# A hybrid attention and convolution layer: the last nine taps of one channel tile move from VectorE to ScalarE products with adding DMAs

## What is computed

```
h    = modulate(rms_norm(x)),  proj = h @ w_in
q, k, v -> 8 heads of windowed attention with 2 key groups, 256 context keys, a sink
u    = ga * sigmoid(gb)                       # 512 channels
u    = silu(layer_norm(depthwise_conv(u)))    # 31 taps, centred, over positions
x    = x + g1 * (concat(attn, u) @ w_out)
x    = x + g2 * ((silu(gate) * val) @ w_down) # gate, val: w_up with 3 taps
shift, scale, gate of both halves: silu(c) @ w_mod + b_mod   (w_mod 1024 x 6144)
```

## Time and profile before

| | |
|---|---|
| median of 3 runs | 1235.33 us |
| the profiled execution | 1237.15 us, its span 1235.3 us |
| mean granted PE clock | 0.964 |
| PE busy | 1159.9 us (94%) |
| DVE busy | 948.4 us (77%) |
| ACT busy | 580.2 us (47%) |
| POOL busy | 315.4 us (26%) |
| head groups 0 to 15 | 243.9 to some 463 us |

### The profile page before, as it was taken

One profiled execution on the slowest core, in us unless ns is written; L12 is line 12 of the kernel. 1 busy time (PEld: TensorE's weight loads), 2 busy tenths in 40 slices (PEclk: granted clock), 3 DMA queues, 4 the chain that ended last, 5 costly groups with the idle time before them and its releaser, 6 DMA issues.

```text
span 1235.3 us, 16863 instructions
## 1 busy us (share of the span) xinstructions
PE 1159.9 (94%) x5837; PEld 962.4 (78%) x5837; DVE 948.4 (77%) x1403; ACT 580.2 (47%) x993; POOL 315.4 (26%) x335
## 2 busy tenths in 40 slices
PE   5799999889999999998799999999999998999997
PEld 1378888788888987786588888788788876888885
DVE  0479988679984454458999999999999967788687
ACT  4452356765545563545443444434444434444441
POOL 2100011134563000000544453635520000002256
PEclk9899999989899879999899999999999998999998
DMA  9322555519999013222445445355342285335352
GB/s 376 109 73 71 130 103 114 143 33 258 266 261 273 2 53 110 105 76 69 154 130 176 152 136 170 120 169 158 131 153 78 76 320 200 103 104 159 102 162 85
DMA packets 102833, 174.90 MB, mean 142 GB/s; under 512 B 9322, under 2 KB 62690, under 8 KB 101748
## 3 DMA queue, kind: packets, MB, share of 16 engines
q1 hardware_dynamic: 84692, 112.04, 27.1%
q0 software_dynamic: 16928, 57.88, 18.9%
q10 hardware_dynamic: 1152, 4.19, 0.9%
HBM read 116.41 MB, written 30.41 MB: 119 GB/s over the span
## 4 chain that ended last, share of the span: by engine, by line
PE 36%; DVE 12%; issue 5%; ACT 4%; DMA 3%; POOL 1%; DVEq 0%; ACTq 0%; SPq 0%; POOLq 0%
PE ps L1527 16%; PE ps L1492 5%; PE ps L1577 5%; PE ps L1578 5%; PE ps L1579 5%; DVE y L1931 2%; DVE w_op L1830 2%; DMA hid<-hid_scratch 2%; DVE w_raw L1848 1%; DVE y L1927 1%; ACT y L1722 1%; ACT w_op L1642 1%; POOL p_all L2099 1%; DVE u L1920 1%; DVE s_sum L1848 1%
## 5 line engine op out<-in xcount | busy, mean ns | idle before, releaser
L1527 PE MATMUL ps<-t_op,w_op 128*128 128x512 f32 x1056 | 247.3, 390 | 2.8 <-issue 0.9
L1527 PEld LDWEIGHTS ps<-t_op,w_op 128*128 128x128 f32 x1056 | 197.7, 188 | 46.3 <-issue 3.2
L1527 PE MATMUL ps<-hx,w_op 128*128 128x512 f32 x792 | 191.8, 396 | 10.1 <-DVE u L1920 6.9
L1527 PEld LDWEIGHTS ps<-hx,w_op 128*128 128x128 f32 x792 | 150.8, 191 | 44.0 <-DVE u L1920 6.5
L1642 ACT ACTIVATE w_op<-w_raw 128x512 fp32r<-128x512 f32 x132 | 80.0, 623 | 196.8 <-DVE w_raw L1848 186.9
L1577 PE MATMUL ps<-dnh,ah 128*128 128x512 f32 x308 | 121.8, 395 | 10.5 <-DVE dnl L1938 10.5
L1578 PE MATMUL ps<-dnl,ah 128*128 128x512 f32 x308 | 121.0, 393 | 0.0
L1579 PE MATMUL ps<-dnh,al 128*128 128x512 f32 x308 | 120.8, 392 | 0.0
L1830 DVE TENSOR_TENSOR w_op<-w_raw,w_op 128x512 fp32r<-128x512 f32 x132 | 101.8, 785 | 10.0 <-ACT w_op L1642 7.7
L1742 ACT ACTIVATE ah<-hid 128x512 fp32r<-128x512 f32 x77 | 48.7, 632 | 112.8 <-PE ps L1579 104.3
L2076 POOL DMA_DIRECT2D wd<-in_w_down x44 | 32.0, 729 | 270.5 <-DVE h_first L1819 193.4
(11 more groups left out here) (288 smaller groups left out, 2411.7 us busy)
## 6 DMA issues: line engine op xcount, KB each, us to landing
w_raw<-in_w_up SPq DMA_DIRECT2D x44, 512.0 KB, 5.2
wm<-in_w_mod SPq DMA_DIRECT2D x32, 512.0 KB, 6.0
sums<-wm POOLq DMA_DIRECT2D x32, 512.0 KB, 7.9
wd<-in_w_down POOLq DMA_DIRECT2D x44, 256.0 KB, 3.3
w_down_sums<-wd POOLq DMA_DIRECT2D x44, 256.0 KB, 2.8
dn_raw<-w_down_sums SPq DMA_DIRECT2D x44, 256.0 KB, 2.7
hid_scratch<-hid SPq DMA_DIRECT2D x20, 512.0 KB, 4.4
hid<-hid_scratch SPq DMA_DIRECT2D x20, 512.0 KB, 5.3
```

Source lines behind the costliest of these rows:

```text
L1527: last = pe.matmul(bank_of(p, s), w_op[p][w][:, k, :], rows_of(p, k, v), start=(start and k == 0 and w == 0 and v == 0), stop=(k == KH - 1 ...
```

## The change

All 31 taps of tile 1 become ScalarE products. The last nine stand in head groups 0 to 3, behind the Exp of the j named in `PROD_AT`, and ahead of `output_high`. DVE keeps one step, the addition of the two sums, in group 5. POOL's stream gets nine more `add_product`, all ahead of the memsets. On SP the wait for taps and join and the first four loads of w_out go ahead of the last round of w_mod.

```diff
         SUM = [cacc[:, AT, :], conv_y[:]]
-        P_BLOCK = 22
+        P_BLOCK = TAPS
+        PROD_AT = {0: (1, 3), 1: (1, 3), 2: (1, 3), 3: (0, 2, 4)}
...
             if n == 0:
                 for r in range(2):
-                    dve.wait_ge(sum_in[r], 16 * (P_BLOCK // 2 - 1))
+                    dve.wait_ge(sum_in[r], 16 * len(range(2 + r, P_BLOCK, 2)))
...
         JOINS = TAPS - P_BLOCK + 1
-        JOIN_AT = ((), (3,), (3,), (3,), (3,), (3,), (3,), (1, 3), (1, 3))
+        JOIN_AT = {5: 3}
...
                         sp.dma_start(wm2[:, a, :], w_mod[0, k * P:(k + 1) * P, sec * D:(sec + 1) * D]).then_inc(wm2_in[a], 16)
+                    if k == KT - 2:
+                        sp.wait_ge(tap_done, NTAP)
+                        sp.wait_ge(join_done, JOINS)
+                        for kk in range(4):
+                            sp.dma_start(wo_raw[:, kk, :], w_out[0, kk * P:(kk + 1) * P, :]).then_inc(wo_in[kk], 16)
                     if k == 0:
...
-                sp.wait_ge(tap_done, NTAP)
-                sp.wait_ge(join_done, JOINS)
-                for k in range(4):
-                    sp.dma_start(wo_raw[:, k, :], w_out[0, k * P:(k + 1) * P, :]).then_inc(wo_in[k], 16)
...
                             exps(n + 1, j)
+                        if j in PROD_AT.get(n, ()):
+                            product(act)
                         if j == 3 and n:
...
-                                if j in JOIN_AT[n]:
+                                if JOIN_AT.get(n) == j:
                                     join_taps(dve, joined)
```

## The result

The changed kernel takes 1242.07 us in the median of 19 executions, the kernel before 1235.26 us in 19 beside it: a ratio of 1.0056 [1.0037, 1.0075], so 0.6% slower, some 7 us (the bracket is the 95% interval of the ratio). The forecast was 1231.4 us in a range of 1226 to 1238. Its profiled execution took 1243.7 us, with a span of 1241.9 us against 1235.3.

A forecast was written before the change was run, and what follows sets the result against it. DVE was taken to set the pace in groups 2, 3, 5 and 7, through joins and stretching beside POOL. With the stream ending last, 5.7 us earlier less 1.8 for a clock fall gave 1235.3 - 3.9 = 1231.4, range 1226 to 1238.

The forecast's parts named there:

- What bounds the kernel: Groups 2, 3, 5 and 7: DVE, busy 10.4 to 13.4 us of 10.9 to 15.2, sets the pace.
- Groups 4 to 8 ... Sum: -10.3: Groups 4 to 8: seven joins leave, one addition comes, 7.7 us; two clock falls gone, some 2.6 us; together -10.3.
- The stretching stays: Groups 4 to 8: DVE is still stretched beside POOL, since the stream then starts with group 4; no gain counted.
- Group 0, +0.6: Group 0: the product at j = 1 costs ACT +1.2 us, less 0.6 for less PE work at half clock.
- Group 1, +0.1: Group 1: the product ahead of output_high costs +0.9 us; DVE's addition and POOL's load leave; together +0.1.
- Group 2, +1.0: Group 2's tail: product on ACT's way +1.1 us, DVE's join leaves; +1.0 taken, bounds -1.8 and +2.3.
- Group 3, +0.2: Group 3: the third product falls into ACT's wait behind the fifth copy; +0.2 us, bounds -1.3 and +3.4.
- The moved stream: POOL's stream starts 29.2 us later, memset at 294.8, length still 137 us, last sum landing at 431.7.
- The stream ends last: Group 13: the stream ends after the groups' 430.7, so DVE's split comes at 432.9, 5.7 us earlier than before.
- rival B: Stream shorter than before by over 2 us, so the groups set the end; gain 6 to 10 us, chance 0.17.
- D: Rival: ACT's chain and clock falls in groups 2 and 3 delay the stream; 2.5 to 5.8 us slower, chance 0.13.
- C: Rival: two clock falls, in group 2 or 3 and behind group 13's wait; gain 0 to 2.4 us, chance 0.24.

The follow-up runs named there:

- x1: The kernel before with the nine DVE joins left out and nothing added: ratio to the kernel before 0.9989, and 0.9960 when run again.
- x13: The kernel before, joins kept, with the nine products also computed but not added, at x10's places: ratio to the kernel before 1.0058.
- x10: The changed kernel without group 0's product at j = 1, products of j = 3 behind output_high and the last copy, three in group 2: 1.0008 against before.
- x4: The changed kernel with the products of j = 3 moved behind output_high and the group's last copy: ratio to the kernel before 1.0024.
- x2: The kernel before, joins kept, with the nine products also computed but not added, at the changed kernel's places: ratio to the kernel before 1.0058.
- x3: The kernel before with POOL's stream waiting for group 3's last copy and the w_out loads moved as in the change: ratio to before 1.0024.
- x11: The kernel before with POOL's stream waiting for group 3's last copy, the w_out loads left as before: ratio to the kernel before 1.0010.
- x5: The changed kernel with stream start and w_out loads as before, the last six additions issued between the stream's steps: ratio to the kernel before 1.0058.
- x6: The changed kernel with the nine products spread over groups 1 to 7, stream early, the addition of the sums in group 8: 1.0122 against before.
- x9: The kernel before with taps 22 to 27 as products in groups 0 to 5, 28 to 30 on DVE, stream early: ratio 0.9970, again 0.9988.

## Why the prediction was wrong

- **What bounds the kernel.** That DVE sets the pace of groups 4 to 8 by the length of its work was wrong. I read DVE's busy time (10.4 to 13.4 us) against PE's floor of 10.0 us in group 12, a group without taps or joins. Groups with taps took 11.5 us in x1 without joins and with the clock full, and 11.3 us in x13 with the joins and the clock at 0.99.
- **"Groups 4 to 8 ... Sum: -10.3"** is the step that failed most. Measured: 65.4 against 68.9, -3.5, and against the second profile of before +2.5; the second profile of the change has 69.1 us. Leaving the joins out, with nothing added anywhere, gives 1.4 to 4.9 us. The 7.7 us of DVE work was counted at full length, and the 2.6 us for two clock falls belonged to one execution. "The stretching stays" missed that its place matters: the opening burst now stands in group 4, 4.8 us of it.
- **Group 0, +0.6.** Measured +0.7 and +1.2. x10, without the product at j = 1, has 12.11 us, within the two profiles of before (12.52, 11.50). Over all profiles group 0 took 13.2 to 13.7 us in the six with that product and 11.4 to 12.6 us in the eleven without it. Right in kind; in size it is near 1.5 us, and the 0.6 taken off for the clock is not to be seen.
- **Group 1, +0.1.** Measured +0.9 and +1.6. I netted the product in front of `output_high` against DVE work that left; but the wait for ACT was the later way, and the DVE work had stood beside it. x4 takes the product out of the way: 13.40, near x1's 13.29.
- **Group 2, +1.0.** Measured +0.9 and +1.6, with the wait at the place named: 1.61 us forecast as "near 1.7", and the fall behind it. **Group 3, +0.2**: 12.65 and 13.50 against 11.32 and 12.18.
- In sum groups 0 to 3 were forecast at +1.9 and came at +3.9 and +6.7, part of it clock. That the products cost 7.2 us with everything else as before (x2) is the other step that failed, and without it there would be hardly a loss: with the joins at 3 us in place of 10.3 and all else as forecast, the sum comes within 2 us of the kernel before. The named part is ACT in front of `output_high`; the other is DVE shifted under POOL's burst. x13 keeps the second without the first: in its profile groups 0 to 3 are 2.5 us shorter than x2's, and the ratio is the same.
- **The moved stream.** Right to some 5 us at each point: memset 296.92 (294.8 forecast), last landing 436.9 (431.7), a length of 140 us (137), full DMA from 302 to 430 (1.01). "**The stream ends last**" was wrong, by the groups and not by the stream: they were to bring DVE's split to 430.7, and it came at 442.71, behind ACT's at 440.95. By my own test, a split behind its copy with no wait, this was rival B's sign, yet with the groups slower and not faster.
- **The rivals.** D had the right mechanism, ACT's chain in groups 2 and 3 with a fall behind it, and the right side. It sent the price through the late stream at group 13 and so let it count from 8.2 us on only; it counts at once, in the groups themselves. C had the clock: the changed kernel has 16.2 and 26.6 us at half clock in groups 2 to 8, against 12.8 and 6.9. By the rule of the Trainium skill in "TensorE: Matmul & The Clock Gate", HAM oscillation, that PE's waits between bursts throttle it again, the trace agrees at the tails of groups 2, 4 and 6 (waits of 1.61, 2.40 and 0.87 us, then 0.57, 0.50 and 0.50), but not at each tail: the earlier trace rows has a wait of 1.30 us with no fall behind it.
- **ACT against DVE.** The product is 1.22 us, the tap 1.28. The price was never in the instruction, but in what stood behind it.
- **"Everything behind group 15 is unchanged and moves with it."** The code is, the time is not: 783.7 us in the first profile and 786.1 us in the changed kernel's, and 782.6 to 789.0 us over all.
- The parts nearly add up: 7.2 for the products, 1.2 to 2.9 for the late stream, 1.4 to 4.9 off for the joins, together +3.5 to +8.7, measured +7. (These are sums of single estimates; their intervals are wider.) But x10, with the same parts at other places, is at +1 where x13 and the late stream would give it the same +3.5 to +8.7. So the products' cost depends on what else moves. The profiles show one way: beside x13's products the early burst stretches DVE in groups 2 and 3 by 6.9 us, where before has 1.9; x10 has its burst in group 4 and pays 3.3 us there, and x3 and x11, with no product at all, pay 3.0. A product that costs nothing on ACT can still move DVE under POOL's burst. Whether that is all of the difference stays open, since x13's one profiled execution was also its second fastest.

## What to carry to other kernels

Before an instruction is moved to an idle engine, look at what stands next in that engine's stream and who waits for it: two kernels with the same nine products, which differ in nothing but their places, are 6 us apart. Then look at what the shift does to the other engines: a move of 0.6 us put two taps under POOL's multiplies. Work taken off the engine that sets the pace is worth only the distance to the next chain, which is found by leaving it out in one run (here 3 us of 11.5). And take no clock fall of a single profile as the kernel's own: profile the unchanged kernel twice first.

## What the runs showed of the hardware

- A DVE tap of 0.74 us took 2.0 to 2.4 us when it started 0 to 0.5 us ahead of POOL's TENSOR_SCALAR of 128x1024 (changed kernel, x2, x13), and a DVE addition of 128x4 1.46 in place of 0.15: about its own time and the whole of POOL's, 1.42 to 1.45. In the kernel before one that started 0.14 us ahead kept its 0.74 us, and POOL's took 1.59; what decides between the two is not shown. Over one group the burst of four cost DVE 1.2 us (before), 3.0 (x3, x11), 3.3 (x10), 4.5 (x13) or 4.8 us (changed kernel).
- The adding DMA of 512 KB between two places of SBUF lands in 4.5 us alone and in 9.4 to 14.4 us beside the full stream (x5, x6, x9), so a ring of two places that never waited before holds ACT for up to 8.7 us.
- The time that PE spends at half clock in the same seven groups of the same kernel was 12.8 and 6.9 us in two executions, 16.2 and 26.6 in the changed one; one group of unchanged code took 23.7 to 28.9 us.
